# Range clears, a deferred wait for stores, and another order in a chunked scan

## What is computed

```python
def step(S, inp):                                  # gated delta rule, a chunk of tokens
    v_new = u_c - einsum(w_c, S)
    o = einsum(qd_c, S) + einsum(qk_c, v_new)
    S = S * exp(gl_c) + einsum(kd_c, v_new)
...
def step(S, inp):                                  # RWKV-7, one token
    Sa = einsum('bhvk,bhk->bhv', S, a_t)
    S = S * w_t + Sa[..., None] * b_t + v_t[..., None] * k_t
    return S, einsum('bhvk,bhk->bhv', S, r_t)
...
for layer in range(DEPTH):
    h = rms_norm(x, norm_mix_pre);  mix = mixer(h)
    x = x + rms_norm(mix, norm_mix_post)
    h = rms_norm(x, norm_ffn_pre)
    x = x + rms_norm(square(relu(h @ w_ff1)) @ w_ff2, norm_ffn_post)
```

## Time and profile before

| | us |
|---|---|
| three timed runs, median (lowest to highest) | 4395.2 (4394.23 to 4397.49) |
| profiled execution, its own time | 4396.1 |
| its span, first to last instruction | 4394.2 |
| scan, from barrier to barrier | 693.6 to 1734.0 |
| first and second feed-forward | 1888.5 to 2794.3 and 3486.4 to 4394.0 |
| TensorE busy | 4116.3 (94% of the span) |
| VectorE, ScalarE, GpSimd busy | 2202.8, 1382.8, 1155.5 |
| mean granted TensorE clock | 0.963 of full speed |

### The profile page before, as it was taken

The page is one execution under the profiler, slowest core; times in us unless marked ns, Lnnn a source line. Parts: engine busy times, 40 slices in busy tenths (PEclk is TensorE's granted clock), DMA queues, the critical chain, the costliest instruction groups (busy, mean ns, idle before and its releaser), DMA issues. The chain is left out here.

```text
span 4394.2 us, 60637 instructions
## 1 busy us (share of the span) xinstructions
PE 4116.3 (94%) x24096; PEld 3573.7 (81%) x24096; DVE 2202.8 (50%) x3149; ACT 1382.8 (31%) x2243; POOL 1155.5 (26%) x643
## 2 busy tenths in 40 slices
PE   7999886999999997989999999789998899999998
PEld 6888765999999997778888888578886788888887
DVE  5643354666656666833333333556663343333334
ACT  3321463434444443421111111435543311111112
POOL 1121264333333332421111111213331211111113
PEclk9999877999999998999999999799999999999999
DMA  4222583121111111411111111300002211111112
GB/s 129 78 91 65 169 303 135 49 68 49 49 63 49 49 54 70 156 49 38 38 38 38 38 38 38 106 7 7 7 1 101 87 37 39 38 38 38 38 38 96
DMA packets 205554, 287.98 MB, mean 66 GB/s; under 512 B 31216, under 2 KB 148272, under 8 KB 205376
## 3 DMA queue, kind: packets, MB, share of 16 engines
q1 hardware_dynamic: 205376, 285.50, 19.7%
HBM read 207.47 MB, written 77.99 MB: 65 GB/s over the span
## 5 line engine op out<-in xcount | busy, mean ns | idle before, releaser
L840 DVE TENSOR_TENSOR top_acc<-top_acc,ffn_down 128x512 f32<-128x512 f32 x600 | 412.6, 688 | 358.3 <-PE ffn_down L111 357.6
L109 PE MATMUL ffn_up<-hT_ffn_high,ffn_w_high 128*128 128x512 f32 (+1 forms) x1536 | 543.8, 354 | 4.9 <-DVE hT_ffn_low L802 4.9
L111 PE MATMUL ffn_up<-hT_ffn_high,ffn_w_low 128*128 128x512 f32 (+1 forms) x1536 | 543.6, 354 | 0.0
L110 PE MATMUL ffn_up<-hT_ffn_low,ffn_w_high 128*128 128x512 f32 (+1 forms) x1536 | 543.4, 354 | 0.0
L109 PE MATMUL ffn_down<-ffn_w_high,ffn_f_high 128*128 128x512 f32 x1280 | 498.6, 390 | 0.0
L110 PE MATMUL ffn_down<-ffn_w_low,ffn_f_high 128*128 128x512 f32 x1280 | 498.3, 389 | 0.0
L111 PE MATMUL ffn_down<-ffn_w_high,ffn_f_low 128*128 128x512 f32 x1280 | 497.9, 389 | 0.0
L829 DVE TENSOR_TENSOR ffn_square<-ffn_relu 128x512 f32<-128x512 f32 (+1 forms) x192 | 146.8, 765 | 640.6 <-ACT ffn_relu L755 640.6
L785 POOL TENSOR_TENSOR ffn_w_low<-up_w_raw,ffn_w_high 128x2048 fp32r<-128x2048 f32 x32 | 147.6, 4612 | 735.0 <-ACT ffn_w_high L761 718.7
L109 PEld LDWEIGHTS ffn_up<-hT_ffn_high,ffn_w_high 128*128 128x128 f32 x1536 | 290.4, 189 | 46.5 <-issue 5.7
L788 POOL TENSOR_TENSOR ffn_w_low<-up_w_raw,ffn_w_high 128x2048 fp32r<-128x2048 f32 x32 | 147.2, 4599 | 673.0 <-ACT ffn_w_high L747 673.0
(11 more groups left out here) (455 smaller groups left out, 8910.9 us busy)
## 6 DMA issues: line engine op xcount, KB each, us to landing
up_w_raw<-in_w_ff SPq DMA_DIRECT2D x64, 1024.0 KB, 5.3
s_tm_both<-prepare_tb SPq DMA_DIRECT2D x20, 512.0 KB, 7.0
s_fm_dir<-prepare_fd SPq DMA_DIRECT2D x20, 512.0 KB, 5.9
scan_tb<-s_tm_both SPq DMA_DIRECT2D x20, 512.0 KB, 3.7
scan_fb<-s_fm_both SPq DMA_DIRECT2D x20, 512.0 KB, 4.7
scan_fd<-s_fm_dir SPq DMA_DIRECT2D x20, 512.0 KB, 5.1
up_w_raw<-s_x SPq DMA_DIRECT2D x20, 512.0 KB, 4.7
top_acc<-in_w_in_even SPq DMA_DIRECT2D x18, 512.0 KB, 5.2
```

The lines of the kernel that those rows point to most:

```text
L109: pe.matmul(out, stationary[0], moving[0], start=start, stop=False)
L110: pe.matmul(out, stationary[0], moving[1], start=False, stop=False)
L111: return pe.matmul(out, stationary[1], moving[0], start=False, stop=stop)
L840: dve.tensor_tensor(a, a, out_of(u), ALU.add).then_inc(added, 1)
```

## The change

It has these parts. `clear_semaphores` sorts the numbers of a stage's semaphores and clears each unbroken run of numbers with one instruction: 26 instead of 387 in the whole program. The stores of ffn0 count on a semaphore that outlives the stage, and SyncE waits for it in norm2. In the preparation's last tile the three gate operations are VectorE's. In the scan's lead-in the constants are split over three semaphores and loaded when they are first needed, the last five behind all tiles; the clearing of `out` is split between VectorE (7 tiles) and GpSimd (3); GpSimd's other clears go behind `g_rows`; ScalarE waits for no constants. And in a turn, five calls change their place: VectorE's `gx(4)` and `k_rows(1)`, TensorE's and ScalarE's first step of quad 2, and the two halves of ScalarE's `g_first`.

```diff
 residual_norm(..., rows_stored=None)
+    if rows_stored is not None:
+        E.made.append(rows_stored)
...
+            if rows_stored is not None:
+                sp.wait_ge(rows_stored, 16 * TILES)
...
 feed_forward(..., stored_later=None)
+    x_stored = stored_later or E.sem("x_stored")
...
-            sp.wait_ge(x_stored, 16 * TILES)
+            if stored_later is None:
+                sp.wait_ge(x_stored, 16 * TILES)
...
 prepare_tokens: SyncE, GpSimd, VectorE
-                sp.wait_ge(s["gated"], n + 1)
+                if n + 1 < TILES:
+                    sp.wait_ge(s["gated"], n + 1)
+                else:
+                    sp.wait_ge(s["last_gated"], 1)
...
+                if n + 1 == TILES:
+                    break
                 pool.wait_ge(s["bonus_out"], n + 1)
...
+            dve.wait_ge(s["bonus_out"], TILES)
+            dve.wait_ge(s["gate_out"], TILES)
+            link(dve.tensor_tensor(tb[j][:, 4, :], tb[j][:, 4, :], ln_b, ALU.add))
+            link(dve.tensor_tensor(tb[j][:, 4, :], tb[j][:, 4, :], tb[j][:, 3, :], ALU.mult))
+            dve.tensor_tensor(tb[j][:, 3, :], tb[j][:, 3, :], ln_g, ALU.mult).then_inc(s["last_gated"], 1)
...
 recurrences, SyncE's lead-in
+            load_gdn(0, 0, 0)
+            for d in range(2):
+                sp.dma_start(outside[d][:, :], ins["c_outside"][d]).then_inc(s["shift_consts"], 16)
...
+            load_gdn(1, 0, 0)
+            for d in range(2):
+                load_dir(d, 0, 0)
+            sp.dma_start(both_levels[:, :, :], ins["c_both_levels"].rearrange("m s t -> s m t")).then_inc(s["consts"], 16)
...
+            for dst, name in ((excl, "c_excl"), (keep, "c_keep")):
+                for d in range(2):
+                    sp.dma_start(dst[d][:, :], ins[name][d]).then_inc(s["consts"], 16)
+            sp.dma_start(head_cols[:, :], ins["c_head_cols"]).then_inc(s["consts"], 16)
...
 recurrences, TensorE
                 pairs(6, KT, "k_pairs", *K_ORDER[1])
+                first(i, 2)
                 pe.wait_ge(s["turned_out"], 4 * i + 4)
                 y(i, 0)
                 g_right(i)
                 pe.wait_ge(s["gxt_joined"], LAST * i + LAST)
                 z(i, 0)
-                first(i, 2)
                 y(i, 1)
...
 recurrences, ScalarE
                 inner(i, 0)
+                x_first(i, 2)
                 y_copy(i, 0)
                 xt_first(i, 2)
-                x_first(i, 2)
...
-                for g in range(2, G):
+                if more:
+                    g_xt_first(i, 1)
+                right_copy(i, 2)
+                if more:
+                    g_x_first(i, 1)
+                for g in range(3, G):
                     right_copy(i, g)
-                if more:
-                    g_first(i, 1)
...
 recurrences, GpSimd's lead-in
-            pool.memset(out[:, :, :], 0.0).then_inc(s["cleared"], 1)
+            pool.memset(out[:, DVE_TILES:TILES, :], 0.0).then_inc(s["cleared"], 1)
+            pool.wait_ge(s["sum_consts"], SUM_CONSTS)
...
             g_rows(0, 0, 1)
+            for q in range(1, Q):
+                pool.tensor_copy(NTc[q][:, :, :], bcm(ident[:, :], GR)).then_inc(s["cleared"], 1)
+            pool.wait_ge(s["consts"], CONSTS)
+            pool.tensor_tensor(first_level[:, :], both_levels[:, 0, :], ident[:, :], ALU.add).then_inc(s["level_made"], 1)
+            pool.wait_ge(s["cleared"], CLEARED)
             g_first(0, 0)
...
 recurrences, VectorE
-            dve.wait_ge(s["consts"], CONSTS)
-            dve.wait_ge(s["cleared"], 9 + RQ)
+            dve.memset(out[:, 0:DVE_TILES, :], 0.0).then_inc(s["cleared"], 1)
+            dve.wait_ge(s["shift_consts"], SHIFT_CONSTS)
...
                 ar(link, i, 1)
-                k_rows(1)
+                gx(i, 0, 4)
                 b_masks(link, i, 0)
-                gx(i, 0, 4)
                 for d in range(2):
                     rests(i, d)
+                k_rows(1)
                 b_masks(link, i, 1)
...
 clear_semaphores
+    numbers = sorted(sem.num for sem in sems)
+    starts = [n for n in numbers if n - 1 not in numbers]
+    ends = [n + 1 for n in numbers if n + 1 not in numbers]
...
-            for sem in sems:
-                sp.sem_clear(sem)
+            for start, end in zip(starts, ends):
+                sp.sem_clear(range(start, end))
```

More of the change, by code:

```diff
@@ L1407, in _ @@
         def _(sp):
-            for dst, name in ((incl, "c_incl"), (excl, "c_excl"), (outside, "c_outside"), (sums, "c_decay_sums"),
-                              (keep, "c_keep")):
-                for d in range(2):
-                    sp.dma_start(dst[d][:, :], ins[name][d]).then_inc(s["consts"], 16)
-            sp.dma_start(both_levels[:, :, :], ins["c_both_levels"].rearrange("m s t -> s m t")).then_inc(s["consts"], 16)
-            sp.dma_start(ones[:, :], ins["c_ones"]).then_inc(s["consts"], 16)
-            sp.dma_start(head_cols[:, :], ins["c_head_cols"]).then_inc(s["consts"], 16)
+            for d in range(2):
+                sp.dma_start(incl[d][:, :], ins["c_incl"][d]).then_inc(s["sum_consts"], 16)
+            sp.dma_start(ones[:, :], ins["c_ones"]).then_inc(s["sum_consts"], 16)
             def load_ar(d, i, o):
@@ L1458, in _ @@
         def _(pe):
-            pe.wait_ge(s["consts"], CONSTS)
-            pe.wait_ge(s["cleared"], 9 + RQ)
+            pe.wait_ge(s["sum_consts"], SUM_CONSTS)
+            pe.wait_ge(s["shift_consts"], SHIFT_CONSTS)
             def g_sums(i, o, d):
@@ L1763, in _ @@
             turn(0, 0, 0, BT)
+            pe.wait_ge(s["cleared"], CLEARED)
             for i in range(TILES):
@@ L1768, in _ @@
         def _(act):
-            act.wait_ge(s["consts"], CONSTS)
             def decay_exp(i, o, d):
@@ L1917, in _ @@
                 pool.memset(S_r[d][:, :, :, :], 0.0).then_inc(s["cleared"], 1)
-            pool.memset(out[:, :, :], 0.0).then_inc(s["cleared"], 1)
-            for d in range(2):
-                last_tile = TILES_P - 1 if d == 0 else TILES_P
-                for name in ("exp_rest", "exp_last"):
-                    pool.memset(rates[name][d][:, last_tile, :], 0.0).then_inc(s["cleared"], 1)
-            for q in range(1, Q):
-                pool.tensor_copy(NTc[q][:, :, :], bcm(ident[:, :], GR)).then_inc(s["cleared"], 1)
-            pool.wait_ge(s["cleared"], 9 + RQ)
-            pool.wait_ge(s["consts"], CONSTS)
-            pool.tensor_tensor(first_level[:, :], both_levels[:, 0, :], ident[:, :], ALU.add).then_inc(s["level_made"], 1)
+            pool.memset(out[:, DVE_TILES:TILES, :], 0.0).then_inc(s["cleared"], 1)
+            pool.wait_ge(s["sum_consts"], SUM_CONSTS)
             def g_rows(i, o, d):
@@ L1994, in _ @@
             g_rows(0, 0, 1)
+            for d in range(2):
+                last_tile = TILES_P - 1 if d == 0 else TILES_P
+                for name in ("exp_rest", "exp_last"):
+                    pool.memset(rates[name][d][:, last_tile, :], 0.0).then_inc(s["cleared"], 1)
+            for q in range(1, Q):
[3 more added lines that the diff above has]
+            pool.wait_ge(s["cleared"], CLEARED)
             g_first(0, 0)
@@ L2192, in _ @@
             assert link.n == DVE_BEFORE, link.n
+            dve.wait_ge(s["consts"], CONSTS)
+            dve.wait_ge(s["cleared"], CLEARED)
             for i in range(TILES):
```

32 lines of the change are left out of this document (20 added, 12 removed).

## The result

The changed kernel takes 4338.44 us (median of four runs, 4330.87 to 4341.3), the kernel before 4395.59 (four runs, 4394.23 to 4397.49): ratio 0.9867, 95% interval 0.985 to 0.9884, a gain of 57.2 us. The forecast was 4327 with a gain of 68.3; the time lies in the range, 11 us above the forecast. It is also, by chance, the figure that rival (a) gives (4338), so the total alone can't tell the two apart; the experiments can. The profiled execution takes 4341.3 us, its span is 4339.5, the mean granted clock 0.965.

What follows compares the result with a forecast made beforehand. The scan was taken as bound by TensorE's queue and its waits, with stage hand-overs also on the path. Gains 22 + 2.3 + 2.5 + 5.5 + 36 = 68.3 us from 4396.1, less 0.9, gave 4327 us; range 4310 to 4350.

Steps and rivals of the forecast that it cites:

- rival (a): Semaphore clears between stages: a clear costs by its members, 10.8 of the 22 us stay, 4338 us; chance 0.12.
- clears: Between stages: 26 clears in place of 387, at 0.063 us a step; gain 22 us, bounds 11.9 and 22.7.
- ffn0's stores: End of the first feed-forward: the wait for the last store moves to the norm behind; gain 2.3 us, bounds 0 and 2.3.
- preparation's last tile: End of the preparation: VectorE does three gate operations instead of GpSimd, one or two stretched; gain 2.5 us.
- lead-in: Start of the scan: shared clearing and reordered constants let GpSimd's first inverse start earlier; gain 5.5 us, bounds 3 and 7.7.
- order of a turn: In the scan's turns: three edits close TensorE's waits; gain 36 us, floor 31.1, ceiling 41, lower bound 15.
- data end at 712.5: Scan's lead-in: large loads finish at 712.5 us because the first big load is issued 4.8 us earlier.
- some 20: Sign in the scan's lead-in: GpSimd's first inverse starts some 20 us after the stage begins, not 26.
- four waits: TensorE's waits at four places per scan turn: 12.2, 10.0, 8.1 and 3.0 us, 31.1 us of it in the ten turns.
- rival (b): Scan turns: waits reopen elsewhere, on VectorE's joins or TensorE's wait for `first(2)`; 15 us instead of 36, 4348; chance 0.13.
- second edit: Scan turn: inverse 2's transpositions go ahead of `y(0)`, their copy ahead of `y_copy(0)`, closing waits of 1.22 and 0.30 us.
- rival (d): Scan turns: slower, as TensorE waits in order for GpSimd's late `first(2)`; 4413 us at 5 us a turn; chance 0.02.

Runs made afterwards that it cites:

- c1_clears: The kernel before with range clears of semaphores alone; 4373.28 us beside 4395.11, ratio 0.9949.
- c3_lead: The kernel before with the scan's new lead-in alone (constants split, memsets shared, other queue order); 4391.71 us, ratio 0.9993.
- c2_turn: The kernel before with the scan's new order within a turn alone; 4360.79 us, ratio 0.9925.
- a3_both: The changed kernel with VectorE's second-unit joins between the two right-hand sides, and GpSimd's first inverse waiting for one constant only; 4329.16 us, ratio 0.9852.
- a1_joins: The changed kernel with VectorE's joins of the second unit put between the two right-hand sides; 4331.3 us, ratio 0.9853.
- t1_gx: The kernel before with one move alone: VectorE's join `gx(4)` ahead of `k_rows(1)` and the first masks; 4383.15 us, ratio 0.9974.
- t3_split: The kernel before with one move alone: ScalarE's `g_first` copied in two halves around `right_copy(i, 2)`; 4389.6 us, ratio 0.9987.
- t2_first: The kernel before with one move alone: inverse 2's transposes ahead of `y(0)` on TensorE, their copy ahead of `y_copy(0)` on ScalarE; 4378.23 us, ratio 0.9962.

## Why the prediction was right, and where its sizes were off

The mechanisms were those of the text, and the time fell in the range. The sum was 11 us too large: 6 of them in the turn, 3.5 in the lead-in. Term by term, forecast against what the runs showed:

| term | forecast | measured | from |
|---|---|---|---|
| clears | 22 | 21.7 to 21.8 | series of clears in the traces; c1_clears |
| ffn0's stores | 2.3 | 2.3 | GpSimd's end to first clear, five kernels |
| preparation's last tile | 2.5 | 2.0 | last product to gate's store |
| lead-in | 5.5 | about 2 | c3_lead; 31.7 to 33.1 against 30.0 us |
| order of a turn | 36 | 30 | c2_turn |
| sum | 68.3 | about 58 | whole: 57.2 |

**Clears.** A step was 0.063 us in the scan's series and 0.061 over all stages, so 361 steps less gave 21.7. A range costs 0.03 to 0.12 us; a member more adds 1.4 ns and not 30, so rival (a) is out.

**Stores.** Nothing else at the barrier waited for open transfers (the text's lower bound of 0), and norm2 hides their landing.

**Preparation.** "One or two are stretched" was right: two were, and GpSimd's products paid 0.45 us for it as well. The rule that the Trainium skill gives (GPSIMD Engine Reference, Specifications: contention on the shared SBUF interfaces when VectorE reads two SBUF operands) agrees with the rows: 1.06 and 1.64 us beside GpSimd, 0.69 behind its end. By itself it would have given 0.2 us; the length of GpSimd's work bounded it.

**Lead-in.** The failed step is "data end at 712.5", which moves the last load by the same 4.8 us as the first. The first large load did go 4.8 earlier (1.7 us into the stage instead of 6.5), as ten of the thirteen constants no longer stand ahead of it. But five of these ten (two of `outside`, two of `sums`, and `both_levels`) only moved in between the loads, so the last load is five places earlier, not ten. Five times 0.48 is 2.4 us. Its issue came 2.6 earlier (700.58, 14.8 into the stage, against 17.4), and the data ended 21.8 us into the stage instead of 24.9, where the text has 19.1. With 2.4 in place of 4.8 the text's own sum gives 1.7 to 3.7; GpSimd's first inverse came 2.9 earlier, 23.3 us into the stage and not "some 20". Slow issues aren't the reason. Three issues ahead of the last load took 2.33, 1.65 and 2.16 us, but the kernel before had such ones too (1.32, 1.12 and this one, the largest):

```profile
707.09 3.71 SPq L1419 DMA_DIRECT2D scan_fb<-s_fm_both  x1
```

The last constant landed 4.9 us behind its issue and 0.9 behind the data, 22.7 into the stage. VectorE's share of the clearing took 6.03 us by its row (the text's 6.3) and held nothing: VectorE's next operation waited for TensorE's sum. The text named the right thing as the limit (the constants, not the clearing of `out`); a3_both shows it by taking it away, which gives 4 us more.

**Turn.** The four waits closed and the text's sizes for them hold: with all closed and none opened (a1_joins) the period falls 3.83 us, the forecast's 3.8, for 3.28 us of waits; a closed wait gave 1.17 times its length in the mean (1.04 in t1_gx, 1.26 in t3_split), close to the 36 over 31.1 that the text took. What was missed is rival (b) in a small form: its wait for VectorE's joins came, at `joins(1)` as the text feared ("within 1 us of being late at `joins(1)` by my count"), but it cost 0.68 us a turn, 6.9 us in all, and not half of the gain. The count took the point as a bound instead of a term, and it missed a cost. The second edit brings TensorE earlier to `y(2)` and `y(3)` by the 1.5 us it saves. With TensorE, GpSimd's masks come earlier too, and they land beside VectorE's right-hand sides, which grow from 0.69 and 0.69 to 1.51 and 0.81: VectorE's chain ahead of the join is 0.94 us longer, where rival (b) has "its own sum there gets 0.8 shorter" (`k_rows` did, but it stands earlier in the turn). The wait is 0.45. So by this count the join would hardly have been late without the stretch; no run has the move without it, so that split is reckoned and not shown. That the move opens the wait is shown by t2_first, and that the second right-hand side ahead of the join is needed for it by a1_joins. TensorE's `first(2)` never waited for GpSimd, so rival (d) had no ground.

**Spread.** Nothing in the text foresaw that single runs of one kernel lie up to 18 us apart. In the twelve profiles the preparation varies most, by 9.7 us. Two rows of the table by stretches, about 100 us into that stage, for the kernel before:

```profile
587.00:607.00 20.00, 15.30 (x68) 10.36 (x68) 9.04 (x11) 10.36 (x22) 12.55 (x9) 0.67 0.85 288
607.00:627.00 20.00, 19.41 (x114) 15.38 (x112) 11.85 (x17) 12.97 (x24) 10.97 (x9) 0.74 0.79 272
```

And the same two stretches of the same code in t1_gx:

```profile
589.00:609.00 20.00, 15.47 (x107) 11.45 (x105) 11.64 (x14) 14.15 (x27) 15.96 (x13) 0.91 0.98 318
609.00:629.00 20.00, 19.05 (x76) 14.38 (x77) 10.61 (x13) 11.26 (x21) 10.09 (x9) 0.52 0.77 264
```

The granted clock, in the column before the DMA share, moves between 0.52 and 0.91 in such a stretch, at other moments in each execution; at 0.52, near the lower level of 1.2 GHz, TensorE is busy 19.05 of 20 us for 76 matmuls. The stage lasts 192.5 to 202.2 us. Whether the clock is the cause, or the loads (share 0.77 to 0.98), was not tried and stays open.

## What to carry to other kernels

Closing a wait in an in-order queue is worth slightly more than the wait, but look next at the engine that already works without a pause behind it: where it is within a microsecond of being late, put the next wait into the sum as a term, and interleave the dependent work on that engine in the same edit (0.68 us a turn here). An edit that brings one engine earlier brings those that wait for it earlier too: ask beside which operations their work then falls (0.94 us on VectorE here). When a queue is reordered, count the places of each transfer by itself, the last one above all. A semaphore that collects several constants makes each reader wait for the last one in the queue; give the one that the critical chain reads its own. And whatever is done member by member between barriers is on the path in full: 387 clears cost 22.8 us, 26 ranges 1.1.

## What the runs showed of the hardware that I had not expected

- A clear of one semaphore and a clear of a long range are the same instruction in the trace (EVENT_SEMAPHORE_RANGE_CLEAR): 25 to 43 ns each for single ones, with 0.061 us from one to the next in the mean, and 30 to 115 ns for ranges. The ranges grow with their members, by about 1.4 ns each (66 ns for 21 members and 76 for 31, in c1_clears).
- Most issues of DMAs on SyncE took 0.32 to 0.48 us, but single large loads took 1.12 to 3.71 us in the lead-in. Small constants issued right behind them, with seven loads still open, took 0.42 to 0.44 again (changed kernel), and in a turn of c3_lead one load took 1.76 right behind a single other. So the number of open loads alone doesn't explain it; the cause is open.
- A clear of 7168 columns took VectorE 6.03 us (0.84 ns a column), GpSimd 2.66 for 3072 (0.87), and 8.63 for the 10240 of the kernel before (0.84). So say the rows. The three of the earlier trace rows on VectorE, 1286 columns in 1.13 us, start 1.35 us apart, which is 1.05 ns a column, so VectorE's rows may be shorter than the time that such a clear holds the engine.
- Moving three operations beside GpSimd cost both sides: VectorE 0.37 and 0.95 us on two of them, GpSimd 0.45 on its pair. In the scan an operation on two SBUF operands took 0.69 alone and 1.51 beside a GpSimd mask, and one with an operand in `scan_ps` took 0.68 with GpSimd busy beside it throughout (L2117 at 1144.34, beside L1954).
